# Two tiles of an output projection multiplied before the first program ends, in banks that the second program takes over

## The reference, cut to what matters

```python
def hybrid_layer(...):                      # layer one
    o_nsa  = nsa_mixer(...) * gate          # channels 0..511 of the mix
    o_rwkv = group_norm(recurrence(...)) * gate   # channels 512..1023
    return h + concat([o_nsa, o_rwkv]) @ w_out

def second_block(x, mem, ...):
    for i in range(2):
        h = rms_norm(x, attn_norm[i]); proj = h @ w_in
        mix = diff_attention(...) if i == 0 else gla_attention(...)
        cross = memory_cross_attention(mem_q, mem, ...)   # rms_norm(mem) @ w_kv
        x = x + concat([mix, cross]) @ w_out[i]
        x = x + conv_ffn(rms_norm(x, ffn_norm[i]), ...)
```

## Time and profile before

| what | value |
|---|---|
| median of 3 executions | 1882.98 us |
| the profiled execution | 1882.68 us, of which the span from first to last instruction 1880.9 us |
| PE, share of the span | 95% (1779.4 us, 11768 matmuls) |
| DVE, ACT, POOL | 51%, 28%, 37% |
| granted TensorE clock, mean | 0.976 |
| last y of layer one to the end of its last rest | 505.6 to 524.2 us |
| first matmul of the second program | 526.4 us |
| wait of PE in the first Rows | 545.0 to 548.6 us |

### The profile page before, as it was taken

The page is one execution under the profiler, slowest core; times in us unless marked ns, Lnnn a source line. Parts: engine busy times, 40 slices in busy tenths (PEclk is TensorE's granted clock), DMA queues, the critical chain, the costliest instruction groups (busy, mean ns, idle before and its releaser), DMA issues.

```text
span 1880.9 us, 28322 instructions
## 1 busy us (share of the span) xinstructions
PE 1779.4 (95%) x11768; PEld 1428.0 (76%) x11768; DVE 955.4 (51%) x1644; ACT 534.1 (28%) x1080; POOL 701.9 (37%) x333
## 2 busy tenths in 40 slices
PE   8999997999879998979999999999999899999999
PEld 5678766877666676767888888886787688888887
DVE  6675247566643546665666552132334366556411
ACT  3111112345414344553422220024322332222100
POOL 4333101000142321334655555462224375555542
PEclk9999999998989999999999999998999899999999
DMA  4222120000132321212222332322112132322322
GB/s 170 77 85 94 27 94 3 3 2 2 35 114 67 127 79 46 74 57 92 90 97 94 101 94 97 101 80 67 60 57 67 46 102 91 101 97 94 101 94 74
DMA packets 43506, 143.54 MB, mean 76 GB/s; under 512 B 5306, under 2 KB 7116, under 8 KB 43251
## 3 DMA queue, kind: packets, MB, share of 16 engines
q1 hardware_dynamic: 43378, 141.73, 23.1%
HBM read 139.07 MB, written 4.08 MB: 76 GB/s over the span
## 4 chain that ended last, share of the span: by engine, by line
PE 63%; DVE 4%; ACT 2%; issue 1%; POOL 1%; DMA 0%; SPq 0%; DVEq 0%; ACTq 0%
PE b_p_bank L206 19%; PE b_p_bank L208 19%; PE b_p_bank L207 19%; POOL b_wlo L187 1%; DVE l_sc L2447 1%; PE b_p_bank L2146 1%; PE b_p_bank L2359 1%; PE b_p_bank L2122 1%; DVE l_mx L2453 1%; PE b_p_bank L2388 0%; PE b_p_bank L2826 0%; PE b_p_bank L1873 0%; PE b_p_bank L2821 0%; PE b_p_bank L2808 0%; PE b_p_bank L2133 0%
## 5 line engine op out<-in xcount | busy, mean ns | idle before, releaser
L187 POOL TENSOR_TENSOR b_wlo<-b_raw,b_whi 128x1024 fp32r<-128x1024 f32 x238 | 580.7, 2443 | 790.6 <-DVE b_whi L180 790.6
L206 PE MATMUL b_p_bank<-b_hi,b_whi 128*128 128x512 f32 x1008 | 408.2, 405 | 12.8 <-PEq L71 6.6
L180 DVE CAST b_whi<-b_raw 128x1024 fp32r<-128x1024 f32 x238 | 185.0, 784 | 449.2 <-PE b_p_bank L208 381.3
L208 PE MATMUL b_p_bank<-b_hi,b_wlo 128*128 128x512 f32 x1008 | 396.6, 393 | 0.0
L207 PE MATMUL b_p_bank<-b_lo,b_whi 128*128 128x512 f32 x1008 | 396.5, 393 | 0.0
L206 PEld LDWEIGHTS b_p_bank<-b_hi,b_whi 128*128 128x128 f32 x1008 | 191.9, 190 | 62.0 <-issue 20.0
L207 PEld LDWEIGHTS b_p_bank<-b_lo,b_whi 128*128 128x128 f32 x1008 | 192.2, 191 | 40.3 <-issue 2.4
L208 PEld LDWEIGHTS b_p_bank<-b_hi,b_wlo 128*128 128x128 f32 x1008 | 191.7, 190 | 41.0
L208 PE MATMUL b_p_bank<-f_mhi,b_wlo 128*128 128x512 f32 x352 | 136.9, 389 | 0.0
L207 PE MATMUL b_p_bank<-f_mlo,b_whi 128*128 128x512 f32 x352 | 136.9, 389 | 0.0
L206 PE MATMUL b_p_bank<-f_mhi,b_whi 128*128 128x512 f32 x352 | 136.9, 389 | 0.0
(11 more groups left out here) (464 smaller groups left out, 2993.2 us busy)
## 6 DMA issues: line engine op xcount, KB each, us to landing
b_raw<-in_w_up SPq DMA_DIRECT2D x88, 512.0 KB, 3.7
b_raw<-in_w_down SPq DMA_DIRECT2D x44, 512.0 KB, 3.6
b_raw<-in_w_in SPq DMA_DIRECT2D x32, 512.0 KB, 3.7
b_raw<-in_w_out SPq DMA_DIRECT2D x24, 512.0 KB, 3.7
b_raw<-in_w_gla SPq DMA_DIRECT2D x22, 512.0 KB, 3.7
b_raw<-in_w_diff SPq DMA_DIRECT2D x20, 512.0 KB, 3.7
b_raw<-in_w_mem SPq DMA_DIRECT2D x8, 512.0 KB, 3.7
all_x<-in_x SPq DMA_DIRECT2D x8, 256.0 KB, 5.4
```

What stands on the lines that cost most here:

```text
L180: self.nc.vector.tensor_copy(self.hi[:, n % SLOTS, :], self.raw[:, n % RAWS, :]).then_inc(self.s_hi, 1)
L187: self.nc.gpsimd.tensor_tensor(self.lo[:, n % SLOTS, :], self.raw[:, n % RAWS, :], self.hi[:, n % SLOTS, :].bitcast(F32), ALU.subtract).th ...
L206: nc.tensor.matmul(acc, lhsT=left[0], rhs=right[0], start=first, stop=False)
L208: return nc.tensor.matmul(acc, lhsT=left[1], rhs=right[0], start=False, stop=last)
```

## The change

Both programs now use the same 8 banks, and the second takes them in another order, so that its first four accumulators are the four banks in which the sparse attention worked. A new generator `Head` multiplies tiles 32 and 33 at the end of the first program: 16 products, 48 matmuls, in 8 steps. They are woven with the four turns "out" on PE, two steps of Head ahead of each turn. `Rows` of the second program begins at its third tile, and the plan has 14 dense steps where it had 22. Tiles 33 and 34 are loaded after the last right-hand side of the recurrence (`s_rhs`) and no longer after the last "y"; tile 32 is rounded once the last "y" is multiplied, ahead of the centring of the last chunk, and tile 33 between "mean" and "var". POOL subtracts both tiles ahead of the four rests of the turns.

```diff
+class Head:
+    def tensor(self, pe):
+        pe.wait_ge(*self.free)
+        for kk in range(4):
+            if kk % 2 == 0:
+                pe.wait_ge(self.ring.s_lo, self.n0 + kk // 2 + 1)
+            self.ready(pe, kk)
+            for b in range(4):
+                mm = product(self.nc, self.banks[b][:, :], self.ring.outputs(self.n0 + kk // 2, kk % 2, b), self.src(kk), kk == 0,
+                             False)
+                if kk % 2 and b == 3:
+                    mm.then_inc(self.ring.s_mm, 1)
+                if b % 2:
+                    yield
 # Rows: tensor, vector, scalar, gpsimd, sync
-        for i in range(self.tiles):
+        for i in range(self.done, self.tiles):
 # second_layer
-    plan = [0] + [1] * 22 + [0] + [1] * 2 + [0] + [1, 0] * 4 + [1] * 4
+    plan = [0] + [1] * 14 + [0] + [1] * 2 + [0] + [1, 0] * 4 + [1] * 4
 # first_layer
-    second = spread(split - chunks, keys) + spread(tail - split, sparse.n - keys) + [1] * (recurrent.last - tail)
+    second = spread(split - chunks, keys) + spread(tail - split, sparse.n - keys)
+    stats, finish = [1] * (recurrent.last - tail), [0, 0, 1] * 4
+    head = Head(nc, ring, over + 8, D4, lambda kk: (c.hi[:, kk, :], c.lo[:, kk, :]),
+                lambda pe, kk: pe.wait_ge(sparse.s_mlo, kk + 1), (sparse.s_m, 4))
 # SP
-            sp.wait_ge(recurrent.s_y, NCH)
+            sp.wait_ge(recurrent.s_rhs, NCH)
             ring.load(sp, over + 8 + 2)
 # PE
-            weave(second, one, sparse.tensor(pe))
+            laid(second + stats, one, sparse.tensor(pe))
+            weave(finish, one, head.tensor(pe))
 # DVE
+            dve.wait_ge(recurrent.s_y, NCH)
             ring.round(dve, over + 8)
-            weave([], one, two)
+            laid([1], one, two)
+            ring.round(dve, over + 9)
+            weave(stats, one, two)
 # POOL
-            ring.rest(pool, over + 8)
-            weave([], one, two)
+            ring.rest(pool, over + 9)
+            weave(stats, one, two)
 # build
-            upper_layers(nc, Memory(nc, st1, "b"), c, k, a, col, x, kt1, vt1, out, base)
+            upper_layers(nc, banks[4:8] + banks[0:4], c, k, a, col, x, kt1, vt1, out, base)
```

More of the change, by code:

```diff
@@ L309, with __init__ @@
 class Rows:
-    def __init__(self, nc, s_stop, i, ring, n0, tiles, banks, src, order, ready, x, outs, s_x):
+    def __init__(self, nc, s_stop, i, ring, n0, tiles, banks, src, order, ready, x, outs, s_x, done=0):
+        self.done = done
         self.nc, self.ring, self.n0, self.tiles, self.banks = nc, ring, n0, tiles, banks
@@ L353, in scalar @@
         work = before()
-        for q in range(4 * self.tiles):
+        for q in range(4 * (self.tiles - self.done)):
             if q % 4:
@@ L385, in add, with __init__ @@
         self.nc.vector.tensor_tensor(self.x[:, o, :], self.banks[b][:, :], self.x[:, o, :], ALU.add).then_inc(self.s_x, 1)
+class Head:
+    n = 8
+    def __init__(self, nc, ring, n0, banks, src, ready, free):
+        self.nc, self.ring, self.n0, self.banks, self.src, self.ready, self.free = nc, ring, n0, banks, src, ready, free
+    def tensor(self, pe):
[11 more added lines that the diff above has]
+                    yield
 class PassedRows:
@@ L3209, in output @@
             rows.append(Rows(self.nc, self.s_stop, i + half, self.ring, n, 4, banks[half], src, order, ready, self.x,
-                             [4 * half + b for b in range(4)], self.s_x))
+                             [4 * half + b for b in range(4)], self.s_x, 2 if w is None and half == 0 else 0))
         return rows
@@ L3399, in third_layer, with upper_layers @@
     return Layer(proj, rows, ff), side, plan
-def upper_layers(nc, m, c, k, a, col, x, kt1, vt1, out, base):
+def upper_layers(nc, banks, c, k, a, col, x, kt1, vt1, out, base):
     c.ring.limit = 10 ** 6
-    u = Upper(nc, c, k, a, col, x, [m.ps(f"bank{i}", [P, 512]) for i in range(8)], base)
+    u = Upper(nc, c, k, a, col, x, banks, base)
     low, side, plan, begin, at_k1, at_v1 = second_layer(u, kt1, vt1)
@@ L3462, in matrices, with first_layer @@
         pe.wait_ge(self.i_ident, 16)
-def first_layer(nc, st, k, a, col, cols, x, c, m):
-    p = Memory(nc, st, "l1")
-    banks = [p.ps(f"bank{i}", [P, 512]) for i in range(8)]
+def first_layer(nc, k, a, col, cols, x, c, m, banks):
     D4, S = banks[0:4], banks[4:8]
@@ L3562, in _ @@
                 pass
-            weave(second, one, sparse.scalar(act))
+            weave(second + stats, one, sparse.scalar(act))
         @block.gpsimd
@@ L3597, in build @@
         with ExitStack() as st1:
[L3598 to L3601, removed]
-            upper_layers(nc, Memory(nc, st1, "b"), c, k, a, col, x, kt1, vt1, out, base)
+            p = Memory(nc, st1, "all")
+            banks = [p.ps(f"bank{i}", [P, 512]) for i in range(8)]
+            base = first_layer(nc, k, a, col, cols, x, c, m1, banks)
+            recycle_semaphores(nc)
+            SPENT.extend(held)
+            upper_layers(nc, banks[4:8] + banks[0:4], c, k, a, col, x, kt1, vt1, out, base)
 def shape_constants():
```

## The result

The changed kernel takes **1890.3 us** in the median of 20 executions (1885.47 to 2000.34), the kernel before 1884.15 us in the same batch (20 executions, 1880.01 to 1895.57). The ratio is 1.0032 [1.0018, 1.0046], slower by 6.0 us (3.4 to 8.7). The forecast was 1887.5 in a range of 1884.0 to 1890.5, "slower" as the likeliest side. The 2000.34 is one execution at a mean granted clock of 0.853, and the ratios leave such executions out. Beyond the Head every line number of after is 26 higher than before (turns L1297, scale L1582, memory L1674 and L1679).

The account below looks back on a forecast made before the run. The second program's head was taken to be bound by the memory's queue, not PE; first program's tail +7.4 and earlier memory issue -2.6 gave +4.8 us on 1882.68, so 1887.5, range 1884.0 to 1890.5.

Parts of the forecast that it names:

- hole before tile 35: Second program's head: PE, done with tile 34, would idle over 8 us before tile 35.
- tile 35 from the program's start: Second program's head: tile 35 ready 19.6 us after the program's first instruction, instead of 22.2.
- The tail, +7.4: End of the first program: Head's matmuls among the turns make it end 7.4 us later (bounds 5.3 and 8.9).
- DVE is held as bounded from above: First program's tail: POOL holds DVE, so tile 32's rounding ends at 507.4 (bounds 506.6 and 507.5).
- The second program's head, -2.6: Second program's start: SP issues the memory's load 2.6 us sooner, so tile 35 comes 2.6 sooner (bounds 1.0 and 2.9).
- Rival C: Second program's head: PE sets the pace, so the change is faster by 4.0 us, 1878.7; chance 0.08.
- I take the queue's order over the chain: Second program's head: tile 35's rounding waits behind the memory's rests in DVE's queue, not for PE.
- the clock falls in it as it does now: PE's hole before tile 35: it grows, but the clock falls as before, at no extra cost.
- the issue's own shift: Memory's load in the second program: the gain equals its earlier issue, 2.6 us, with no loss in transfer.
- rival B: Memory's transfer piles up behind three tiles, low clock reaches the second quarter: +7.9, 1890.6; chance 0.12 with Rival D.
- Rival A: First program's tail: clock stays high through the 4.3 us hole, DVE not held: +2.7, 1885.4; chance 0.20.
- Rival D: First program's tail: Head doesn't run in the hole, all 48 matmuls lengthen the tail, 11 us; counted within 0.12.

Follow-up runs that it names:

- c2: The changed kernel, unaltered, timed and profiled a second time against the kernel before; ratio 1.0032 [1.0014, 1.0051].
- e8: The changed kernel with tiles 32 and 33 rounded only behind the recurrence's last statistics sum; ratio 1.0033 [1.0016, 1.0050] to the kernel before.
- e5: The changed kernel with all 8 Head steps behind the four turns; ratio 1.0044 [1.0029, 1.0059] to the kernel before.
- e1: The kernel before with tile 35 rounded and subtracted ahead of the memory's splits and rests; ratio 0.9973 [0.9954, 0.9993].
- e6: The kernel before with the memory's load issued ahead of tiles 35 to 37; ratio 0.9979 [0.9961, 0.9996].
- c1: The kernel before, unchanged, timed against itself and profiled again; ratio 0.9996 [0.9975, 1.0017].
- e9: The kernel before with only the banks swapped for the second program, nothing moved; ratio 1.0000 [0.9981, 1.0018].
- e2: The changed kernel with tiles 35 and 36 rounded and subtracted ahead of the memory's splits and rests; ratio 0.9989 [0.9970, 1.0008] to the kernel before.
- e3: The changed kernel with the turns put before the Head's later quarters; ratio 1.0017 [0.9991, 1.0042] to the kernel before.
- e4: The changed kernel with the memory's load issued ahead of tiles 35 to 37; ratio 1.0005 [0.9988, 1.0021] to the kernel before.
- e7: The changed kernel with turns before the Head's later quarters, memory loaded first and tile 35 rounded early; ratio 0.9975 [0.9958, 0.9993] to the kernel before.

## Why the prediction was right

Measured, in the order of its own list:

| step | predicted | after | c2 |
|---|---|---|---|
| Head's first matmul behind the last "y" | 4.3 | 4.26 | 4.27 |
| first turn | 9.5 | 9.65 | 9.24 |
| end of the last turn | 22.4 | 23.1 | 22.5 |
| second program's first instruction | 28 | 28.65 | 28.0 |
| memory's issue behind that | 3.7 | 3.6 | 3.6 |
| hole before tile 35 | over 8 | 6.35 | 7.29 |
| tile 35 from the program's start | 19.6, "about 20" | 18.05 | 18.1 |

Two terms made the sum, and both hold.

**The tail, +7.4.** The second program starts at 28.65 and 28.0 where the kernel before has 20.7 in all three profiles, +7.6 in the mean. It is made up as the prediction had it: a first quarter at half clock in front of turn 1, then PE as the bound, with turns 4.03 us apart, the first pair 4.29 (12 x 0.23 + 1.15 = 3.9 was reckoned). The last turn's end, 537.04 + 1.15 - 515.05 = 23.1, is 0.7 late: 0.15 from turn 1, 0.1 at each turn's distance, and the low clock's reach into turn 1, 1.44 us instead of 1.15.

DVE is held as bounded from above: the rounding of tile 32 takes 1.52 us instead of 0.68 and ends 0.5 after POOL's L821; the centring L1572 takes 2.34 instead of some 0.4 and ends 0.3 after POOL's L187; in e8 two scales take 3.97 beside POOL instead of 1.41. The Trainium skill, SBUF — State Buffer, section "SBUF: two separate sides", has VectorE and GpSimd exclude each other for whole instructions of this kind; the trace agrees. For it and for the roundings a first turn that waits for the scale alone comes 2.8 us late (e5), but in after the matmuls ahead of the turn end 0.4 later still, so the scale decides only where those are done a little sooner (c2).

**The second program's head, -2.6:** the issue comes 2.8 sooner. Rival C is refuted by e1 and e6: an edit of DVE's queue, or of SP's, closes PE's hole and wins 4 to 5 us. "I take the queue's order over the chain" was the decision on which the sign hung; the row of DVE's wait in rows 6 named a wait that had long been granted (e1's rounding at 532.12), next to an instruction that happened to end then.

**What lies between the +4.8 and the time.** In round numbers, after and c2 against c1 and e9, from the last "y" to the squares:

- the tail +7.6, the memory's issue -2.8, together +4.8 as in the forecast;
- transfer to first split: 7.15 and 7.3 against 7.1 and 6.3, +0.5;
- tile 35's start to the squares: 15.9 and 16.6 against 15.3 and 15.4, +0.9. In all kernels the same matmuls, at half clock for some 3 us in c1 and e9, for 4.8 in after (0.85 over 15.9) and 6.2 in c2 (0.53 over 6.6).

Together +6.2, where +6.0 (3.4 to 8.7) was timed. The prediction had the last two at nothing ("the clock falls in it as it does now"; the issue's own shift). These four traces alone would call that an error of 1.4 us, but the other traces don't bear it out. The transfer behind the tiles has a mean of 7.5 us in four traces of the old order (before, c1, e9, e1: 6.3 to 8.6) and of 7.5 in six of the new (after, c2, e2, e3, e5, e8: 7.15 to 7.8). And from tile 35 to the squares it is 15.4 in e5 and e8 as well, behind holes of 7.2 and 6.9 us, just as in c1 and e9 behind 1.8. So neither rival B's pile-up of 1.6 us nor a dearer fall of the clock behind the longer hole is shown; what the pairs differ by is of the size by which executions of one kernel differ.

**What was luck.** The sum was made from one execution that had a slow transfer and 5.9 us of low clock behind its hole. Against it the same stretch grew by only 62.58 - 59.44 = 3.1; against the mean of before, c1 and e9 it grew by 5.2. What held are the two differences; that they met the time from such a base is in part luck. The time itself, 1890.3, is 2.8 above the forecast and only 0.2 inside the range: 1.5 of the 2.8 is that the kernel before had a median of 1884.15 in this batch, where the sum starts at 1882.68.

**Rival A** (clock stays up, DVE not held) did not occur. In c2, e4 and e7 the clock stayed up through the hole but fell with the Head's first matmuls, and DVE was held; the first turn came 0.4 us sooner than in after, not 2.1. **Rival D** did not occur: in after, c2, e2, e3, e4 and e7 the Head starts 4.3 us after the last "y". e5 shows that it would have cost little more.

What stays open: upstream and downstream of the stretch the traces of one kernel differ among themselves by up to 9 us up to the last "y" (505.6 to 515.05) and about 3 us behind the squares, with the granted clock. Behind the squares the five traces without the Head have 1314.7 to 1315.9 us to the span's end, the eight with it 1314.6 to 1318.6, a mean 1.5 more; whether that is chance or the change's is not shown. The 1.5 us of disagreement in the list above is of that size.

## What to carry to other kernels

Work moved into an engine's idle time pays only if that engine is late where the work was, and if the place it goes to holds nothing that others wait for: here 48 matmuls left a stretch in which PE had 2 to 4 us to spare, and went in front of four turns that end a program. Where a chain of waits changes engine at a wait, look up whether that wait had been granted long before, and follow the order of the queue instead; a rounding moved ahead of eight other instructions was worth more than 48 matmuls moved. And profile the kernel before more than once when the answer is a few microseconds: the one execution read here had a transfer 1.5 to 2.3 us longer than the next two, and a hole twice as long.

## What the runs showed of the hardware

- **A short hole costs clock behind it.** Holes of 1.8 us (c1, e9) and 2.6 (e4) kept 1.00 to their end, and the matmuls behind them then ran at a mean of 0.54 to 0.66 for 3.2 to 4.6 us, which is some 1.5 us lost (c1: 13 matmuls in 4.54 us, at 0.23 each they are 3.0); without the hole (e1) there is no fall. So the hole of 1.8 us costs some 3.3, and e1 and e6 win twice what PE's wait was. Behind e7's hole of 0.91 us the clock stayed at 1.00.
- **A longer hole was not always the dearer one.** Tile 35 to the squares took 15.4 us behind holes of 1.8 (c1, e9), 6.9 (e8) and 7.2 us (e5), 15.9 behind 6.35 (after), and 16.5 and 16.6 behind 3.65 (before) and 7.3 (c2). The low clock behind the hole was 5.9 us where the hole was 3.65, and 4.8 where it was 6.35.
- **Around a hole of 4.3 us the clock falls at one of two times** in the same kernel. In after it fell in the hole, to a mean of 0.91, and the first matmul of the Head took 0.76 us; in c2 it was 1.00 up to the Head's start, the first matmul took 0.59, and the first 12 had a mean of 0.63. The difference is 0.8 us on those 12.
- **The memory's load** takes 4.8 to 4.9 us when issued first (e4, e6, e7), 6.3 to 8.6 behind the tiles, and differs by 2.3 us between executions of the same instructions (before 8.6, e9 6.3).
